# A fifth turn of the down-projection's second group as seven block products

## The chip, the core and the metric

The kernel runs on one core of one Trainium2 chip. The time is the device time of one execution in microseconds (us). The engines named below are TensorE (PE: matmuls; PEld: its weight loads), VectorE (DVE), ScalarE (ACT), GpSimd (POOL) and SyncE (SP, which issues most loads). Stores to DRAM are issued by SP and ACT and carried by 16 DMA engines.

## What is computed

The reference is two residual blocks over 256 tokens of width 2048, in float32. The change touches only the very last product of the second block, the down-projection:

```python
h2 = rmsnorm_2(x, norm2_g[l])
u = causal_dwconv(jnp.einsum('bsd,df->bsf', h2, w_up[l]), conv_w[l], conv_b[l])
u_gate, u_val = u[..., :D_FF], u[..., D_FF:]
x = x + jnp.einsum('bsf,fd->bsd', jax.nn.silu(u_gate) * u_val, w_down[l])
```

Here `f = silu(u_gate) * u_val` is 256 x 5632, `w_down` is 5632 x 2048, and the result is added to `x` and stored.

## The kernel before

**Precision.** Every float32 operand is split into a high and a low part in the type that TensorE multiplies fast (fp32r). A product is three matmuls: high by high, high by low, low by high. ScalarE writes the high part of a piece of weights (`high_of_chunk`, `w_hi`, L1014), VectorE subtracts it from the piece to get the low part (`low_of_chunk`, `w_lo`, L1432).

**Items.** The weights come as pieces of 256 rows by 512 columns (512 KB), and the whole kernel is one list, `ITEMS`, each item with one split into `w_hi` and `w_lo`. These have four slots: item n is split when item n-4 has been multiplied (ACT waits for it). VectorE and ScalarE go through the same loop of steps; step n of a phase prepares item n+4 (`split`) and then does what else is to be done at that step. Below, the items of the phase `down` are counted from 0 (0 to 108 before the change).

**The down phase.** It has two groups of 1024 output columns (column blocks 0 and 1, then 2 and 3). The 5632 rows are 11 turns of 512 rows. A plain turn is 4 items, C0 to C3, of 12 matmuls each: 128 tokens by 128 rows by 512 columns, for 2 row tiles, 2 token tiles and 3 parts (`wide_chunk`, L653). A turn by products takes the 2 x 2 blocks of the piece (two token tiles, two halves of rows, two column blocks) by Winograd's scheme with 7 products instead of 8. Each product is an item of 6 matmuls (`wide_product`, L676 and L680); they are written P1 to P7 here. It needs:

- the four weight blocks in buffers of their own (`load_block` on SP), of which VectorE makes four differences (`block_sum`, L1437, 128x1024 each);
- sums of the turn's rows of `f`: VectorE adds high and low part (L1519), makes four sums (L1522 to L1525), ScalarE takes their high part two steps later (`sums_high`, L1074), VectorE their low part three steps later (`sums_low`, L1474). `SUMS_AT` has the step for each such turn, `SUM_TURNS` the turn, `down_wide` the place of the parts;
- P1, P5, P6 and P7 are summed over all turns of a group in four PSUM banks of their own (`XS`). After P6 of the group's last turn by products, ScalarE copies the sum of P1 (`first_product`, L1112) and VectorE adds all of them up and into `x` (`add_products`, L1670 to L1680: four steps with two instructions of 128x512 each, the first step being that of P6). The results of the other products and of the plain turns are in `GG`.

A turn by products is interleaved with a plain one, in the order `MIXED`:

```python
MIXED = (1, "C0", 5, 7, "C1", 6, 3, "C2", 4, 2, "C3")
```

`(8, 6)` in `WIDE_STEPS` is such a mixed stretch of 11 items and 90 matmuls: turn 8 plain, turn 6 by products. `(7, None)` is a plain turn. Before the change, the second group is items 53 to 108: (3, 0) 53 to 63, (7, None) 64 to 67, (4, 1) 68 to 78, (5, 2) 79 to 89, (8, 6) 90 to 100, turn 9 plain 101 to 104, turn 10 plain 105 to 108. The stretches of the profile that are shown below begin with items 68, 79, 90 and 101.

**The end.** When the last item that writes a column block is done, VectorE adds the block to `x` one item later (L2018), and ACT issues its store of 512 KB (L1415). For column block 2 that is after item 106. For column block 3 the last item does its first token tile first; VectorE adds it (L2030) and SP stores 256 KB (L535), then the second tile in two halves (L2034), stored with 128 KB each by ACT (L1417) and SP (L537).

**Places.** `f_hi` has 4 KB for each turn from y+0 on, `f_lo` from y+44 KB on; the sums of turn 6 lie where turn 3 was.

Of the kernel before, what the change touches and what calls it, by code (L numbers as in the profile page):

```python
# [58 lines left out]
for _name, _w in (("a_norm", KD), ("norm1", KD), ("norm2", KD), ("b_s", GROUPS),  # L59
# [29 lines left out]
    "out1": (((0, None), (1, None), (6, None), (2, 4), (3, 5), (7, None)),  # L89
             ((0, None), (1, None), (2, 4), (3, 5), (6, None), (7, None))),  # L90
    "down": (((3, None), (4, None), (8, None), (9, None), (5, 0), (6, 1), (7, 2), (10, None)),
             ((3, 0), (7, None), (4, 1), (5, 2), (8, 6), (9, None), (10, None))),
    "gm0": (((0, 3), (1, 2)),),
    "gm1": (((0, None), (1, 3), (2, None)),),
    "out2": (((0, None), (2, 1), (3, None)),) * 2,
}


SUM_TURNS = {"v": (3, 2), "out1": (4, 5), "down": (0, 1, 2, 6), "gm0": (3, 2), "out2": (1,)}


SUMS_AT = {"v": (4, 8), "out1": (1, 4), "down": (3, 6, 9, 64), "gm0": (-8, -5), "out2": (-7,)}

PLAIN = ("C0", "C1", "C2", "C3")
MIXED = (1, "C0", 5, 7, "C1", 6, 3, "C2", 4, 2, "C3")
# [57 lines left out]
def product_item(phase, g, turn, p):  # L163
    return ITEM_AT[Item(phase, g, p, turn, None, None)]
# [6 lines left out]
def last_by_products(phase, g):  # L171

    return [turn for name, group, turn in QUADS if (name, group) == (phase, g)][-1]
# [17 lines left out]
def sum_slot(phase, turn):  # L191

    return SUM_TURNS["gm0" if phase == "gm1" else phase].index(turn)


def sums_ahead(phase):

    return sum(len(turns) for name, turns in SUM_TURNS.items() if FIRST_ITEM[name] < FIRST_ITEM[phase])


def own_ahead(phase, g=0):

    return sum((FIRST_ITEM[name], group) < (FIRST_ITEM[phase], g) for name, group in GROUPS_BY_PRODUCTS)
# [59 lines left out]
def build(nc, x, x_tokens, stream, w_s, params, gain_rows, final_rows, gate_w, identity, consts, out):  # L263

    kib = 1024
# [23 lines left out]
    class Wide:  # L289
# [3 lines left out]
        def __init__(self, sb, name, blocks, hi, lo, rows, sums, u):  # L293
# [98 lines left out]


    down_wide = Wide(sb, "d", [("mix", 0), ("mix", 4 * kib), ("y", 88 * kib), ("y", 92 * kib)],
                     [("h", 0), ("h", 4 * kib), ("h", 8 * kib), ("y", 12 * kib)],
                     [("h", 12 * kib), ("h", 16 * kib), ("h", 20 * kib), ("y", 56 * kib)], ("h", 24 * kib), ("h", 28 * kib),
                     ("h", 24 * kib))
    out1_wide = Wide(sb, "o", [("mix", 0), ("mix", 4 * kib), ("x", 12 * kib), ("x", 4 * kib)],
                     [("h", 8 * kib), ("h", 12 * kib)], [("h", 24 * kib), ("h", 28 * kib)], ("h", 0), ("h", 16 * kib),
# [51 lines left out]
    sem = Sems()  # L451
# [20 lines left out]
    with block:  # L472
# [520 lines left out]
        def _(act):  # L993
# [75 lines left out]
            def sums_high(phase, n):  # L1069

                if n - 2 in SUMS_AT[phase]:
                    i = SUMS_AT[phase].index(n - 2)
                    act.wait_ge(sem["sums_ready"], sums_ahead(phase) + i + 1)
                    activation(wide[phase].sums_hi[i][:], wide[phase].sums[:], ACT.Copy).then_inc(sem["sums_hi_ready"], 1)  # L1074

            def first_product(phase, n):

                for name, g in GROUPS_BY_PRODUCTS:
                    if name != phase:
                        continue  # L1080
                    turn = last_by_products(phase, g)
                    if n == product_item(phase, g, turn, 6):
                        act.wait_ge(mm_done, product_item(phase, g, turn, 1) + 1)
                        if phase == "out1" and g == 0:

                            act.wait_ge(sem["v_lo_ready"], GROUPS)
                        elif phase == "out1":

                            act.wait_ge(sem["own_read"], own_ahead(phase, g))
                            act.wait_ge(sem["sq_ready"], 4)  # L1090
                        elif phase == "gm0":

                            act.wait_ge(sem["m_done"], M_HEADS)
                        elif phase == "gm1":

                            act.wait_ge(sem["merged_turned"], 2)
                        elif phase == "out2" and g == 0:

                            act.wait_ge(mm_done, FIRST_ITEM["out2"])
                        elif phase == "out2":  # L1100
                            act.wait_ge(sem["own_read"], own_ahead(phase, g))
                        elif phase == "v":

                            act.wait_ge(sem["x_sq_ready"], 2)
                            act.wait_ge(group_read[0], g)
                        elif g == 0:

                            act.wait_ge(sem["sums_lo_ready"], sums_ahead(phase) + 3)
                        else:
                            act.wait_ge(sem["own_read"], own_ahead(phase, g))  # L1110
                            act.wait_ge(sem["sums_lo_ready"], sums_ahead(phase) + 4)
                        activation(wide[phase].p1[:], XS[:, 0, :], ACT.Copy).then_inc(sem["p1_ready"], 1)  # L1112

            def v_taken(q):
# [23 lines left out]
            for n in range(items_of("v")):  # L1138
                for q in range(2):
                    if n == half_end("v", 0, q):  # L1140
                        v_taken(q)
                split("v", n)
                if n == 0:
                    in_high(3, 8, 12)
                if n == 1:
                    in_high(4, 12, 16)
                if n in (3, 6):
                    t = n // 6
                    act.dma_start(x_first[:, t, :], x_tokens[:, t, :]).then_inc(sem[f"x_first_in{t}"], 16)
                if n == 4:  # L1150
                    act.dma_start(ident[:], identity).then_inc(sem["ident_in"], 16)
                sums_high("v", n)
                if n in (11, 12):
                    t = n - 11
                    act.wait_ge(sem[f"x_first_in{t}"], 16)
                    activation(x_junk[:, t, :], x_first[:, t, :], ACT.Square,
                               accum_out=n_sum[:, t:t + 1]).then_inc(sem["x_sq_ready"], 1)
                if n == 12:
                    act.dma_start(ws_t[:], w_s).then_inc(sem["ws_in"], 16)
                first_product("v", n)  # L1160
                if n in gelu_at:
                    act.wait_ge(sem["scale_ready"], 1)
                    v_gelu(gelu_at[n])
                if n - 1 in gelu_at:
                    v_squares(gelu_at[n - 1])
# [44 lines left out]
            for n in range(items_of("out1")):  # L1210
                split("out1", n)
                if n == 0:
                    act.wait_ge(sem["v_lo_ready"], GROUPS)
                    act.dma_start(xt[:], x_tokens).then_inc(sem["x_again"], 16)
                    act.dma_start(final_row[:], final_rows).then_inc(sem["final_in"], 16)
                sums_high("out1", n)
                if n == 4:
                    y_high(GROUPS - 1)
                first_product("out1", FIRST_ITEM["out1"] + n)
                for q in range(2):  # L1220
                    at = n - out1_second - 1 - 3 * q
                    if at == 0:
                        act.wait_ge(sem["x_turned"], q + 1)
                        gained_high(norm_mid, q, TR)
                    if at in (1, 2):
                        squares(q, at - 1)
# [101 lines left out]
            for p in range(2):  # L1328
                gm, pa, pm = f"gm{p}", f"pa{p}", f"pm{p}"
                for n in range(items_of(gm)):  # L1330
                    split(gm, n)
                    if p and n == 1:
                        merged_high(1)
                    first_product(gm, FIRST_ITEM[gm] + n)
                for n in range(8):
                    split(pa, n)
                    if n in (1, 3):
                        h = n // 2
                        act.wait_ge(group_read[h], group_of(gm, h)[2])
                        by_token(gate_m[h], gate_m[h], ACT.Tanh, scale_half).then_inc(sem["gate_m_ready"], 1)  # L1340
                for n in range(8):
                    split(pm, n)
                    if n == 6:
                        merged_high(2 * p)
                    if p:
                        sums_high("out2", n - 8)
# [73 lines left out]
        def _(dve):  # L1420
# [51 lines left out]
            def low(to, of, hi, count, value, after):  # L1472
                dve.wait_ge(sem[count], value)
                return v.tensor_tensor(to, of, hi.bitcast(F32), ALU.subtract).then_inc(sem[after], 1)  # L1474
# [38 lines left out]
            def sums_of_rows(phase, n, a_hi, a_lo):  # L1513

                if n in SUMS_AT[phase]:
                    i = SUMS_AT[phase].index(n)
                    at_i = slice(4 * SUM_TURNS[phase][i], 4 * SUM_TURNS[phase][i] + 4)
                    rows, sums = wide[phase].rows, wide[phase].sums
# [8 lines left out]
            def sums_low(phase, n):  # L1527
                if n - 3 in SUMS_AT[phase]:
                    i = SUMS_AT[phase].index(n - 3)
                    low(wide[phase].sums_lo[i][:], wide[phase].sums[:], wide[phase].sums_hi[i][:], "sums_hi_ready",  # L1530
                        sums_ahead(phase) + i + 1, "sums_lo_ready")
# [600 lines left out]
```

## Time and profile before

| | us |
|---|---|
| median of 3 runs | 2097.87 |
| lowest and highest | 2097.71, 2098.06 |
| the profiled execution: its own time | 2097.71 |
| the profiled execution: span from first to last instruction | 2095.9 |
| TensorE busy, VectorE busy, ScalarE busy (of the span) | 2089.8, 1506.6, 1112.4 |

How to read it: the profile is of one execution. Matmuls are pipelined, so that their shown duration (0.39 us) is longer than the distance from one to the next; the rate is read from the distance of their starts. A row of the timeline has the start, the duration, the engine, the line of the kernel, the operation, output and inputs and their count; behind it in brackets stands how long the engine was idle before it and what ended that. Times are from the start of the span.

### The profile page before, as it was taken

The page shows a single profiled execution, that of the slowest core. Times are in us where ns is not written, and L with a number is a line of the kernel's source. Part 1 is how long each engine was busy: PE and PEld are TensorE (multiplying, and loading weights), DVE is VectorE, ACT ScalarE, POOL GpSimd, SP SyncE. Part 2 cuts the span into 40 slices and gives each one's busy share as a digit, 9 for nine tenths or more (in the row PEclk, how much of TensorE's full clock was granted, in tenths as well). Part 3 has the DMA queues.
Part 4 walks back from the last instruction along what each step waited for, and adds up shares of the span by engine and source line. Part 5 has one row for each costly group of instructions (what it writes and reads, how often), then busy time and mean ns, then how long its engine had stood idle before and what let it go on. Part 6 is the DMA issues. An engine that isn't in the chain of part 4 may idle for free.

```text
span 2095.9 us, 25218 instructions
## 1 busy us (share of the span) xinstructions
PE 2089.8 (100%) x10000; PEld 1750.1 (84%) x10000; DVE 1506.6 (72%) x1702; ACT 1112.4 (53%) x1314; POOL 17.5 (1%) x17
## 2 busy tenths in 40 slices
PE   9999999999999999999999999999999999999999
PEld 7888888888888887888888888888888888888887
DVE  7987656655787754665669678867777777779986
ACT  6765444444456544555455454555555555555553
POOL 0000000000000000100000000000000000000000
PEclk9999999999999999999999999999999999999999
DMA  8665555555764555544465656556556566556663
GB/s 337 210 200 175 198 187 187 194 187 189 272 214 157 194 194 171 177 155 153 150 210 181 221 169 208 167 185 192 187 185 195 183 192 190 181 181 232 224 203 133
DMA packets 111957, 404.40 MB, mean 193 GB/s; under 512 B 12512, under 2 KB 13280, under 8 KB 111328
## 3 DMA queue, kind: packets, MB, share of 16 engines
q1 hardware_dynamic: 109440, 394.66, 57.1%
q10 hardware_dynamic: 2400, 8.14, 1.0%
q8 instruction: 79, 1.29, 0.3%
q14 instruction: 38, 0.31, 0.0%
HBM read 400.65 MB, written 2.10 MB: 192 GB/s over the span
## 4 chain that ended last, share of the span: by engine, by line
PE 96%; DVE 3%; ACT 1%; DMA 0%; issue 0%; ACTq 0%; DVEq 0%
PE g L556 37%; PE g L653 23%; PE xs L581 8%; PE g L581 8%; PE xs L676 5%; PE xs L585 4%; PE g L585 4%; PE g L680 4%; DVE w_lo L1432 1%; PE xs L604 1%; PE xs L713 1%; ACT w_hi L1014 0%; PE xs L833 0%; DMA xf<-in_x 0%; PE xs L830 0%
## 5 line engine op out<-in xcount | busy, mean ns | idle before, releaser
L1432 DVE TENSOR_TENSOR w_lo<-raw,w_hi 128x1024 fp32r<-128x1024 f32 x659 | 803.4, 1223 | 492.6 <-ACT w_hi L1014 486.9
L1014 ACT ACTIVATE w_hi<-raw 128x1024 fp32r<-128x1024 f32 x659 | 697.4, 1059 | 756.6 <-PE g L556 411.7
L556 PE MATMUL g<-w_hi,mid_both 128*128 128x512 f32 x1024 | 326.7, 394 | 0.0
L556 PE MATMUL g<-w_hi,in_both 128*128 128x512 f32 x1024 | 318.8, 390 | 0.1
L556 PEld LDWEIGHTS g<-w_hi,in_both 128*128 128x128 f32 x1024 | 192.2, 188 | 40.3 <-DVE v_all L1564 0.5
L556 PEld LDWEIGHTS g<-w_hi,mid_both 128*128 128x128 f32 x1024 | 192.3, 188 | 39.6
L556 PE MATMUL g<-w_lo,mid_both 128*128 128x512 f32 x512 | 199.4, 389 | 0.0
L556 PE MATMUL g<-w_lo,in_both 128*128 128x512 f32 x512 | 199.2, 389 | 0.0
L581 PE MATMUL g<-mlp_both,w_hi 128*128 128x512 f32 x704 | 176.8, 393 | 0.0
L581 PE MATMUL xs<-mlp_both,w_hi 128*128 128x512 f32 x704 | 176.3, 392 | 0.0
L581 PEld LDWEIGHTS g<-mlp_both,w_hi 128*128 128x128 f32 x704 | 126.5, 189 | 22.8
L581 PEld LDWEIGHTS xs<-mlp_both,w_hi 128*128 128x128 f32 x704 | 126.6, 189 | 22.6
L653 PE MATMUL g<-w_hi,in_both 128*128 128x512 f32 x352 | 112.6, 390 | 1.3 <-DVE w_lo L1500 1.0
L556 PEld LDWEIGHTS g<-w_lo,in_both 128*128 128x128 f32 x512 | 96.1, 188 | 19.7
L556 PEld LDWEIGHTS g<-w_lo,mid_both 128*128 128x128 f32 x512 | 96.3, 188 | 19.1
L585 PEld LDWEIGHTS g<-mlp_both,w_lo 128*128 128x128 f32 x704 | 96.2, 190 | 7.0
L585 PEld LDWEIGHTS xs<-mlp_both,w_lo 128*128 128x128 f32 x704 | 96.0, 190 | 6.9
L585 PE MATMUL g<-mlp_both,w_lo 128*128 128x256 f32 x704 | 98.3, 282 | 0.0
L585 PE MATMUL xs<-mlp_both,w_lo 128*128 128x256 f32 x704 | 98.2, 282 | 0.0
L653 PE MATMUL g<-w_hi,f_hi 128*128 128x512 f32 x240 | 93.7, 390 | 0.2
L653 PE MATMUL g<-w_hi,f_lo 128*128 128x512 f32 x240 | 93.4, 389 | 0.0
L653 PE MATMUL g<-w_lo,f_hi 128*128 128x512 f32 x240 | 93.4, 389 | 0.0
(404 smaller groups left out, 3044.3 us busy)
## 6 DMA issues: line engine op xcount, KB each, us to landing
raw<-in_stream SPq DMA_DIRECT2D x659, 512.0 KB, 3.5
d_block<-in_stream SPq DMA_DIRECT2D x28, 512.0 KB, 4.6
o_block<-in_stream SPq DMA_DIRECT2D x24, 512.0 KB, 4.7
v_block<-in_stream SPq DMA_DIRECT2D x20, 512.0 KB, 4.4
gm_block<-in_stream SPq DMA_DIRECT2D x12, 512.0 KB, 5.1
x_first<-in_x_tokens ACTq DMA_DIRECT2D x2, 1024.0 KB, 6.8
gain_row<-in_gain_rows SPq DMA_DIRECT2D x8, 256.0 KB, 3.5
xt<-in_x_tokens ACTq DMA_DIRECT2D x1, 2048.0 KB, 8.0
```

The lines of the kernel that those rows point to most:

```text
L556: ins = mm(G[buf][:, t, :], a[:, kt, at_t], w[:, slot, j * COLS:(j + 1) * COLS], start=(kt == 0 and n == 0), stop=(last and j == ROWS_PER_ ...
L581: mm(UP[buf][:, b, :, :], w_hi[:, slot, j * COLS + b * P:j * COLS + (b + 1) * P], a_both[:, :, kt, :], start=(kt == 0), stop=False, skip_g ...
L585: ins = mm(UP[buf][:, b, 0, :], w_lo[:, slot, j * COLS + b * P:j * COLS + (b + 1) * P], a_both[:, 0, kt, :], start=False, stop=(last and j ...
L604: ins = turn(TR[:, b, t * P:(t + 1) * P], of[:, t, b * P:(b + 1) * P], ident[:])
L653: ins = mm(GG[:, bank, :], a[:, kt, t * P:(t + 1) * P], w[:, slot, half_chunk(j)], start=n == 0 and opens(item, bank), stop=ended and n == ...
L676: ins = mm(XS[:, own[p], :], a, w[:, slot, half_chunk(j)], start=first and opens_own(item), stop=last and j == 1 and n == 2, skip_group_ch ...
L680: ins = mm(GG[:, RESULT_OF[p], :], a, w[:, slot, half_chunk(j)], start=first and opens(item, RESULT_OF[p]), stop=False, skip_group_check=True)
L713: ins = mm(SV[:, t, :], w[:, t, :], a[:, t, :], start=(n == 0), stop=(n == 2))
L1014: activation(w_hi[:, n % RING, :], of[:], ACT.Copy).then_inc(hi_ready, 1)
L1432: v.tensor_tensor(w_lo[:, n % RING, :], of, w_hi[:, n % RING, :].bitcast(F32), ALU.subtract).then_inc(lo_ready, 1)
```

## The change

Turn 9 of the second group is computed as seven block products, interleaved with turn 10 in one mixed stretch of 11 items: items 101 to 111 are P1, C0, P5, P7, C1, P6, P3, C2, P4, P2, C3. The sums of turn 9's rows are made by VectorE at step 70, which is inside the mixed stretch (4, 1), and their parts go where turn 7's rows of `f` lie (y+28 KB and y+72 KB). Turn 9 becomes the last turn by products of the group, and so the own products are added up after its P6 (item 106) instead of after turn 6's (item 95). The last item that writes column block 2 is now item 110. ScalarE's copy of P1's sum waits for the fifth low part of sums, since it lies over the place where they are made.

```diff
@@ -89,17 +89,17 @@
     "down": (((3, None), (4, None), (8, None), (9, None), (5, 0), (6, 1), (7, 2), (10, None)),
-             ((3, 0), (7, None), (4, 1), (5, 2), (8, 6), (9, None), (10, None))),
+             ((3, 0), (7, None), (4, 1), (5, 2), (8, 6), (10, 9))),
...
-SUM_TURNS = {"v": (3, 2), "out1": (4, 5), "down": (0, 1, 2, 6), "gm0": (3, 2), "out2": (1,)}
-
-
-SUMS_AT = {"v": (4, 8), "out1": (1, 4), "down": (3, 6, 9, 64), "gm0": (-8, -5), "out2": (-7,)}
+SUM_TURNS = {"v": (3, 2), "out1": (4, 5), "down": (0, 1, 2, 6, 9), "gm0": (3, 2), "out2": (1,)}
+
+
+SUMS_AT = {"v": (4, 8), "out1": (1, 4), "down": (3, 6, 9, 64, 70), "gm0": (-8, -5), "out2": (-7,)}
...
@@ -392,8 +392,8 @@
     down_wide = Wide(sb, "d", [("mix", 0), ("mix", 4 * kib), ("y", 88 * kib), ("y", 92 * kib)],
-                     [("h", 0), ("h", 4 * kib), ("h", 8 * kib), ("y", 12 * kib)],
-                     [("h", 12 * kib), ("h", 16 * kib), ("h", 20 * kib), ("y", 56 * kib)], ("h", 24 * kib), ("h", 28 * kib),
+                     [("h", 0), ("h", 4 * kib), ("h", 8 * kib), ("y", 12 * kib), ("y", 28 * kib)],
+                     [("h", 12 * kib), ("h", 16 * kib), ("h", 20 * kib), ("y", 56 * kib), ("y", 72 * kib)], ("h", 24 * kib), ("h", 28 * kib),
                      ("h", 24 * kib))
...
@@ -1108,7 +1108,7 @@
                             act.wait_ge(sem["own_read"], own_ahead(phase, g))
-                            act.wait_ge(sem["sums_lo_ready"], sums_ahead(phase) + 4)
+                            act.wait_ge(sem["sums_lo_ready"], sums_ahead(phase) + 5)
                         activation(wide[phase].p1[:], XS[:, 0, :], ACT.Copy).then_inc(sem["p1_ready"], 1)
```

## Rows read from the trace of the kernel before

**Rows 1.** The page: granted clock in 40 slices, and the chain that ended last, by engine.

```profile
PEclk9999999999999999999999999999999999999999
...
PE 96%; DVE 3%; ACT 1%; DMA 0%; issue 0%; ACTq 0%; DVEq 0%
```

**Rows 2.** Busy time by stretch: length, then each engine's, clock, DMA share, GB/s.

```profile
2009.24:2030.09 20.85, 20.70 (x91) 16.81 (x90) 19.09 (x18) 11.65 (x12) 0.00 (x0) 1.00 0.57 202
2030.09:2050.49 20.40, 20.40 (x91) 16.89 (x90) 17.75 (x16) 11.57 (x11) 0.00 (x0) 1.00 0.62 206
2050.49:2070.89 20.40, 20.40 (x91) 16.89 (x90) 19.40 (x20) 11.94 (x12) 0.00 (x0) 1.00 0.35 117
2070.89:2092.66 21.77, 21.77 (x97) 17.83 (x95) 10.84 (x11) 5.30 (x5) 0.00 (x0) 1.00 0.33 108
```

**Rows 3.** VectorE in order of time, 2005 to 2027: start, duration, instruction.

```profile
2005.30 1.22 DVE L1519 TENSOR_TENSOR d_rows<-f_hi,f_lo 128x1024 f32<-128x1024 f32 x1
...
2008.15 1.22 DVE L1432 TENSOR_TENSOR w_lo<-raw,w_hi 128x1024 fp32r<-128x1024 f32 x1
...
2015.09 1.22 DVE L1432 TENSOR_TENSOR w_lo<-raw,w_hi 128x1024 fp32r<-128x1024 f32 x1
...
2018.69 1.22 DVE L1432 TENSOR_TENSOR w_lo<-d_block,w_hi 128x1024 fp32r<-128x1024 f32 x1
2019.82 1.22 DVE L1432 TENSOR_TENSOR w_lo<-raw,w_hi 128x1024 fp32r<-128x1024 f32 x1
2020.96 2.36 DVE L1432 TENSOR_TENSOR w_lo<-d_block,w_hi 128x1024 fp32r<-128x1024 f32 x2
...
2026.01 1.23 DVE L1432 TENSOR_TENSOR w_lo<-d_block,w_hi 128x1024 fp32r<-128x1024 f32 x1 [1.49 <-ACT w_hi L1014]
```

**Rows 4.** TensorE in order of time: items 71 to 72, 75 and 96.

```profile
2015.83 0.39 PE L676 MATMUL xs<-w_hi,d_sums_lo 128*128 128x512 f32 x1
2016.36 0.50 PE L653 MATMUL g<-w_hi,f_hi 128*128 128x512 f32 x1
...
2021.94 0.39 PE L653 MATMUL g<-w_hi,f_hi 128*128 128x512 f32 x1
...
2061.38 0.39 PE L680 MATMUL g<-w_hi,d_sums_hi 128*128 128x512 f32 x1
```

**Rows 5.** ScalarE in order of time: the high part of the sums.

```profile
2008.27 1.06 ACT L1074 ACTIVATE d_sums_hi<-d_sums 128x1024 fp32r<-128x1024 f32 x1 [0.41 <-DVE d_sums L1525]
```

**Rows 6.** VectorE in order of time: the additions, and the last results.

```profile
2063.88 0.68 DVE L1670 TENSOR_TENSOR d_u<-xs,d_u 128x512 f32<-128x512 f32 x1
...
2065.20 1.22 DVE L1432 TENSOR_TENSOR w_lo<-raw,w_hi 128x1024 fp32r<-128x1024 f32 x1
2066.34 0.68 DVE L1673 TENSOR_TENSOR d_u<-xs,d_u 128x512 f32<-128x512 f32 x1
...
2071.26 0.68 DVE L1679 TENSOR_TENSOR d_u<-xs,d_u 128x512 f32<-128x512 f32 x1
...
2072.82 3.50 DVE L1432 TENSOR_TENSOR w_lo<-raw,w_hi 128x1024 fp32r<-128x1024 f32 x3
...
2092.86 0.76 DVE L2034 TENSOR_TENSOR xw<-g,xw 128x256 f32<-128x256 f32 x2 [0.67 <-PE g L653]
```

**Rows 7.** The end: stores, last matmul, and stretches with DMA share and GB/s.

```profile
2088.68 0.54 ACTq L1415 DMA_DIRECT2D out<-xw  x1
...
2092.43 0.39 PE L653 MATMUL g<-w_hi,f_lo 128*128 128x512 f32 x1
...
2093.64 0.34 SPq L537 DMA_DIRECT2D out<-xw  x1
...
2089.50:2090.00 0.50, 0.50 (x4) 0.42 (x3) 0.00 (x0) 0.00 (x0) 0.00 (x0) 1.00 0.22 86
2090.00:2090.50 0.50, 0.50 (x4) 0.42 (x3) 0.00 (x0) 0.00 (x0) 0.00 (x0) 1.00 1.04 393
...
2095.00:2095.50 0.50, 0.00 (x0) 0.00 (x0) 0.00 (x0) 0.00 (x0) 0.00 (x0) 1.00 0.02 4
```

## The prediction

> **What bounds the kernel now.** I read the page first, for its clock line and its chain by engine [rows 1]: the clock stands at its top level throughout, and 96% of the chain that ended last is TensorE. Then the stretches of the down phase [rows 2], cut where its matmuls begin: a mixed stretch of 90 matmuls takes 20.40 us and the last 96 plain ones take 21.77 us, so a 512-column matmul costs 0.2267 us, one behind the other. Only the stretch from 2009.24, also 90 matmuls, takes 20.85 us. The timelines say why [rows 3, 4]: VectorE ran without a pause from the row sums at 2005.30 on, the low part of item 72 began at 2015.09, and its first matmul could start only at 2016.36, 0.53 us after the one before it. So TensorE sets the time, except where VectorE has more to do than TensorE's time over the same items: there VectorE's order decides. Therefore I went through VectorE's timeline at the three places where the change puts or moves its work, and then through the end [rows 5 to 7].
>
> **What the change does to each part.**
>
> *Matmuls.* Turn 9 of the second group had 4 items of 12 matmuls and gets 7 of 6: 6 fewer. 6 x 0.2267 = **-1.36 us** [rows 2]. That is the whole gain; the whole stretch of turns 9 and 10 goes from 96 matmuls to 90.
>
> *Splits and block differences.* 3 more items mean 3 more high parts on ScalarE (1.06 us) and 3 more low parts on VectorE (1.22 us); there are 4 block differences (1.22 us) besides. All are prepared during items 97 to 107. The same set was prepared for turn 6 out of the stretch before it, and the stretches from 2030.09 and 2050.49 both take 20.40 us [rows 2], with no time lost. VectorE is 17.75 us busy in the first of the two, which carries just this load. I cost them at nothing; the cover is TensorE's 20.40 us. Turn 6's stretch becomes lighter by the additions that leave it (eight instructions, [rows 6]) and heavier by turn 9's preparation. If VectorE's start-to-start time of 1.14 us did not hold there, 15 operations of 1.22 us would still be 18.3 us, below 20.40.
>
> *Loads.* Four 512 KB blocks come as blocks instead of as ring rows: same bytes. They are issued by SP behind items 93, 96, 98 and 99, as in the stretches before. Nothing else stands on SP's queue there but the remaining ring loads. I take zero for it.
>
> *The sums of rows at step 70.* This is the first time that they stand inside a mixed stretch. Step 70 prepares the low part of item 74, and the sums come before that of item 75. Before, these two stand at 2018.69 and 2019.82 [rows 3]. The sums and their four small operations take from 2005.30 to 2008.15, 2.85 us until the next low part [rows 3]. So item 75's low part starts at 2019.82 + 2.85 = 2022.67. From the start of a low part to the matmul that waits for it are 1.27 us (2015.09 to 2016.36), so item 75 starts at 2023.94. It started at 2021.94 [rows 4]: **2.00 us late**. Behind the shorter stall the matmuls also ran slow for a moment: the stretch lost 0.45 us [rows 2], of which the gap is 0.53 - 0.23 = 0.30; the remaining **0.14 us** I add again. No idle time of VectorE can take up any of it: it has none before this point, and its next is 1.49 us ahead of 2026.01, which is too late.
>
> The two waits that come with it: ScalarE's high part of the sums starts 2.97 us after the sums began (2008.27 against 2005.30, [rows 5]), so at 2022.79; queued behind it is item 77's high part, ready at about 2024.9, when VectorE arrives for item 77's low part (2022.67 + 2 x 1.14 = 2024.95). VectorE's low part of the sums (1.14 us) stands between items 77 and 78 and item 79's low part comes at about 2028.4 instead of 2026.01, 2.4 us later, while TensorE is 2.14 us later. That 0.25 us is covered by VectorE's lead in the next stretch, which lost nothing [rows 2]. The sums are ready 28 items before turn 9 needs them. The place y+28k is free: turn 7's rows were last read by item 67, which ended at 2009.24.
>
> *The additions of the own products.* The eight additions move from turn 6's items 95 to 98 to turn 9's items 106 to 109. Before, they lay under 12 following items; now only 5 items follow. With the end of P6 as the zero (2061.38 before, [rows 4]): the first addition starts at +2.50, its pair lasts 1.32, a low part 1.14 [rows 6]. Item 111's low part is the last, since no item follows it. So the third pair starts at +2.50 + 1.32 + 1.14 + 1.32 = +6.28, where two low parts no longer push it back, the fourth at +7.61, and from its start to the next operation are 1.56 (2071.26 to 2072.82): +9.17. Only then comes the addition of column block 2. That block is now finished by item 110, not two plain items before the end, so its addition too (1.22) is at the very end. Then block 3's first tile (+10.31, after the 1.14 of start-to-start) and its two halves from +10.9; they need 0.78 us until the last store is issued (2092.86 to 2093.64, [rows 6, 7]): +11.7. The last matmul starts at +1.36 + 2.72 + 1.36 + 1.36 + 2.49 = +9.29. Before, the last store was issued 1.21 us after the start of the last matmul (2092.43 to 2093.64); now it is 2.4 us: **1.20 us** more. Item 111's low part ends at about +5, its matmuls start at +6.80, so VectorE does not hold up TensorE here.
>
> *The stores.* Before, block 2's store (512 KB) was issued at 2088.68 and long done when the others began. Now it is issued at about +10.4, next to the 256 KB and two of 128 KB. A store runs at 393 GB/s with the DMA engines wholly busy [rows 7], so they do not overlap, they share. 1.05 MB take 2.71 us. The data of the 512 KB store began about 1.2 us after its issue (86 GB/s in the half microsecond to 2090.00 is its last 0.11 us); so from +11.6 to +14.3. Without the store of block 2 in the way the last data would end as before, some 1.4 us behind the last issue (all but nothing moves after 2095.00), at +13.1. **1.25 us** more; by the bound from below, if the order of the queues lets the short stores slip between, 0; by the one from above, all of 1.36 (the store's 512 KB). I take 1.25, because the end waits for all of them and the bytes have to pass.
>
> That the ACT and SP queues share is also what the Trainium skill says ("DMA: Bandwidth & Descriptors", Issuing engines are not separate DMA queues): they run on the same 16 engines. By its 436 GB/s (same page, Anatomy of one DMA) the 1.05 MB would take 2.4 us and the sum would be 0.3 us lower, an estimate; the trace's 393 decides.
>
> **Sum.** -1.36 + 2.00 + 0.14 + 1.20 + 1.25 = **+3.2 us** on the profiled execution (span 2095.9, its own time 2097.71): 2100.9. The median of the three runs is 0.16 above that execution: **2101.0 us**, 0.15% slower. The bound of what a measurement can tell here is 0.2%, 4.2 us: so no measurable change, on its slow side.
>
> **The rivals.**
>
> *The stores do not collide* (below 0.3 us). For it: the 512 KB store is issued some 1.3 us ahead of the last. Against it: DMA share at 1.0 and more during each store [rows 7]. Then +1.95: 2099.8. Chance 0.17.
>
> *VectorE hides the sums: the other side.* One mechanism, at item 75: if its low part were 2.85 us or more ahead of its matmuls, nothing would stall. It is 0.85 us ahead (low part from 2019.82, usable at 2021.09, matmuls at 2021.94). Even then only the 2.14 us go: +1.1 (2098.9) with the end as worked out, and -1.36 (2096.5) if the end is hidden as well. For it speaks only that VectorE is idle in the plain stretches; against it [rows 3]. Chance 0.05. Neither is faster by 4.2 us.
>
> *The clock falls behind the stall.* The 0.3 us gap left the clock at 1.00 in its stretch [rows 2], and no row shows a gap of 2 us. If TensorE fell from 2.4 to 1.2 GHz, a matmul would take 0.45 us, and each item of 12 done at that level costs 2.7 us more: one item gives 2103.7, over the bound. The Trainium skill ("TensorE: Matmul & The Clock Gate", HAM oscillation) says that a TensorE left waiting long enough is throttled; by its rule a gap as short as this, with full work around it, leaves the clock alone. Chance 0.04.
>
> *The backlog is carried on.* If VectorE's 1.14 us for the low part of the sums is not covered by what it gains on TensorE before item 83, there is a second stall of up to 1.1 us: 2102.1. Against it the 17.75 us busy of 20.40 in the next stretch. Chance 0.06.
>
> *The change does what it says and no more is lost than the gain* (an end that hides the additions, stall as worked out): +0.8, 2098.7. Against it [rows 6]: VectorE's additions cannot start before P6. Chance 0.04.
>
> **How the numbers follow.** The forecast itself has 0.64: the stall and the end are each read from an instance of the same operations, and their errors are some 0.3 us each, so its own range is 2100.3 to 2101.7. The range of 8 in 10 leaves out the hidden sums, the clock and half of the backlog's case: 2099.3 to 2102.1. More than 4.2 us slower is reached by the clock's case and by errors of 1 us upward, together 0.10. Faster by more than 4.2 us has no case, 0.01. The rest is 0.89.
>
> **What will show it.** In the stretch of turns (4, 1): 20.85 + 2.14, about 23.0 us, the wait of the matmuls of item 75 for the low part about 2 us, clock 1.00. The next two stretches 20.40 each. The last 90 matmuls 20.4 us without a gap. Between the start of the last matmul and the end of the span 5.9 us instead of 3.5; VectorE busy without a pause from P6 to the last store; the stores side by side. The prediction is wrong if the stall at item 75 is below 1.5 us, if another one follows, or if the start of the last matmul is less than 4.7 us ahead of the end of the span.

## The result and the profile after

The changed kernel took 2101.54 us in the median of 15 runs (2101.26 to 2103.24), the kernel before 2097.92 us (2097.71 to 2098.21, 15 runs). The ratio is 1.0021, with a 95% interval of 1.0014 to 1.0027: slower, by 0.14% to 0.27%. No run of the one kernel overlaps with one of the other. The median is 3.6 us above, and the forecast was 3.2. But the runs do not lie around their median. Sorted, in us:

```
2101.26 2101.33 2101.44 2101.49 2101.53 2101.54 2101.54 2101.54
2102.71 2102.93 2103.00 2103.09 2103.22 2103.24 2103.24
```

Eight runs have a mean of 2101.46, seven of 2103.06: two levels, 1.6 us apart. The ratio of the medians is 1.0017; the mean over all 15 is 2102.21, 0.20% above before, at the 0.2% that the prediction took as its bound. The profiled execution (its own time 2101.26, span 2099.2) is of the lower level, so it shows only the part that the sum describes.

The stretches of the changed kernel, cut at the first matmuls of items 68, 79, 90 and 101 and at the end of the last item (length, then the busy time of PE, PEld, DVE, ACT and POOL with their instructions, clock, DMA share, GB/s); they answer to [rows 2]:

```profile
2009.13:2032.11 22.98, 21.00 (x91) 16.73 (x90) 22.61 (x24) 12.47 (x13) 0.00 (x0) 1.00 0.55 183
2032.11:2052.51 20.40, 20.40 (x91) 16.89 (x90) 17.85 (x16) 11.58 (x11) 0.00 (x0) 1.00 0.64 206
2052.51:2072.91 20.40, 20.40 (x91) 16.89 (x90) 17.75 (x16) 11.56 (x11) 0.00 (x0) 1.00 0.64 206
2072.91:2093.31 20.40, 20.40 (x91) 16.70 (x89) 19.23 (x21) 8.75 (x9) 0.00 (x0) 1.00 0.00 1
```

Turns 9 and 10 take 20.40 us instead of 21.77: the gain is there, all of it. The next two stretches are full. The first, (4, 1), grew from 20.85 to 22.98 us, with VectorE busy 22.61 of them. VectorE's timeline there (low part of item 74, the sums, low part of item 75):

```profile
2018.56 1.22 DVE L1432 TENSOR_TENSOR w_lo<-d_block,w_hi 128x1024 fp32r<-128x1024 f32 x1
2019.69 1.22 DVE L1519 TENSOR_TENSOR d_rows<-f_hi,f_lo 128x1024 f32<-128x1024 f32 x1
...
2022.54 1.22 DVE L1432 TENSOR_TENSOR w_lo<-raw,w_hi 128x1024 fp32r<-128x1024 f32 x1
```

and TensorE's, the last matmul of item 74 and the first of item 75:

```profile
2021.59 0.39 PE L680 MATMUL g<-w_hi,d_sums_lo 128*128 128x512 f32 x1
2023.82 0.50 PE L653 MATMUL g<-w_hi,f_hi 128*128 128x512 f32 x1 [1.83 <-DVE w_lo L1432]
```

The sums push the low part back by 2.85 us, and the matmul starts 1.28 us after the low part's start. Between the two matmuls are 2.23 us where 0.23 would be: 2.00 us lost, a stall of the matmuls. The clock of this stretch is 1.00, but the 12 matmuls of item 75 take 2.85 us (2023.82 to 2026.67) instead of 2.72: the 0.13 us behind the stall.

The end, as a timeline of all engines but the weight loads:

```profile
2092.13 0.69 DVE L1680 TENSOR_TENSOR xw<-xw,d_u 128x512 f32<-128x512 f32 x1
...
2092.97 1.23 DVE L2018 TENSOR_TENSOR xw<-g,xw 128x1024 f32<-128x1024 f32 x1
2093.09 0.39 PE L653 MATMUL g<-w_hi,f_lo 128*128 128x512 f32 x1
2094.11 0.68 DVE L2030 TENSOR_TENSOR xw<-g,xw 128x512 f32<-128x512 f32 x1
2094.22 0.54 ACTq L1415 DMA_DIRECT2D out<-xw  x1
2094.71 0.75 DVE L2034 TENSOR_TENSOR xw<-g,xw 128x256 f32<-128x256 f32 x2
...
2095.48 0.34 SPq L537 DMA_DIRECT2D out<-xw  x1
```

The last matmul starts at 2093.09. VectorE is only then at the addition of column block 2, and the last store is issued 2.39 us later, against 1.21 before [rows 7]. From there to the end of the span it takes another 3.7 us, against 2.3. The stretches behind it show the four stores side by side (the last three columns: clock, DMA share, GB/s):

```profile
2095.25:2095.50 0.25, 0.00 (x0) 0.00 (x0) 0.20 (x1) 0.00 (x0) 0.00 (x0) 1.00 0.24 82
2095.50:2096.00 0.50, 0.00 (x0) 0.00 (x0) 0.00 (x0) 0.00 (x0) 0.00 (x0) 1.00 1.01 385
...
2097.50:2098.00 0.50, 0.00 (x0) 0.00 (x0) 0.00 (x0) 0.00 (x0) 0.00 (x0) 1.00 1.02 342
2098.00:2098.50 0.50, 0.00 (x0) 0.00 (x0) 0.00 (x0) 0.00 (x0) 0.00 (x0) 1.00 0.58 193
```

The DMA engines are full for 2.8 us without a break.

So the lower level was explained from the trace. Open were the upper level, and whether each part is what it seems. Three theories of the upper level: TensorE's clock falls behind the stall in some executions (the rival that the prediction gave 0.04); the four stores at the end cost more in some executions; something ahead of the down phase.

### The profile page after: what moved, and what is told of

Its sections match the earlier page's. It is cut to its first block, busy times and chain, and to the rows that moved or that the text cites. A ratio compares the mean times of both kernels' runs of the same rounds, so it can differ in the third digit from the quotient of the medians.

```text
span 2099.2 us, 25230 instructions
## 1 busy us (share of the span) xinstructions
PE 2089.6 (100%) x9994; PEld 1749.8 (83%) x9994; DVE 1518.2 (72%) x1715; ACT 1116.2 (53%) x1318; POOL 17.5 (1%) x17
## 4 chain that ended last, share of the span: by engine, by line
PE 95%; DVE 3%; ACT 1%; DMA 1%; issue 0%; DVEq 0%; ACTq 0%
PE g L556 37%; PE g L653 22%; PE xs L581 8%; PE g L581 8%; PE xs L676 5%; PE xs L585 4%; PE g L585 4%; PE g L680 4%; DVE w_lo L1432 1%; PE xs L604 1%; PE xs L713 1%; ACT w_hi L1014 1%; PE xs L833 0%; DMA raw<-in_stream 0%; DVE d_block L1437 0%
## 5 line engine op out<-in xcount | busy, mean ns | idle before, releaser
L1014 ACT ACTIVATE w_hi<-d_block 128x1024 fp32r<-128x1024 f32 x56 | 59.4, 1062 | 63.2 <-PE g L653 42.8
L653 PE MATMUL g<-w_hi,f_hi 128*128 128x512 f32 x224 | 87.6, 391 | 2.0 <-DVE w_lo L1432 1.8
L653 PE MATMUL g<-w_lo,f_hi 128*128 128x512 f32 x224 | 87.2, 389 | 0.0
```

Source lines behind the costliest of these rows:

```text
L653: ins = mm(GG[:, bank, :], a[:, kt, t * P:(t + 1) * P], w[:, slot, half_chunk(j)], start=n == 0 and opens(item, bank), stop=ended and n == ...
L1014: activation(w_hi[:, n % RING, :], of[:], ACT.Copy).then_inc(hi_ready, 1)
```

## The experiments

In the figures below "tail" is the time from the start of the last matmul to the end of the span, in the profiled execution: 3.50 us before, 6.15 us after. All ratios are against the kernel before on the same chip.

**e1: the changed kernel again.** No edit.

> The changed kernel once more, for its two levels: 8 of its 15 runs took 2101.3 to 2101.5 us, 7 took 2102.7 to 2103.2. Clock theory: TensorE's clock falls for a moment behind the 2 us stall at item 75 in some executions; both levels come again, 1.7 us apart, and a trace of the upper one shows a granted clock below 1.00 between items 75 and 85 and nowhere else before the last matmul. Store theory: the upper level comes from the four stores that share the DMA engines at the end; a trace of the upper one shows its 1.7 us behind the last matmul, and matmuls at 0.2267 us throughout.

Median 2101.84 (2101.46 to 2103.19, 11 runs), ratio 1.0019 (1.0010 to 1.0028). Eight runs from 2101.46 to 2102.09, three from 2102.91 to 2103.19. Two levels again, but the profiled execution was of the lower one, so the trace of an upper one was still missing.

**e2: turn 9's sums at step 60.** The sums of turn 0, at h+0 and h+12 KB, are read last by item 59; the place is free from then on.

```diff
-"down": (0, 1, 2, 6, 9)
+"down": (0, 1, 2, 9, 6)
-"down": (3, 6, 9, 64, 70)
+"down": (3, 6, 9, 60, 64)
-[("h", 0), ("h", 4 * kib), ("h", 8 * kib), ("y", 12 * kib), ("y", 28 * kib)],
-[("h", 12 * kib), ("h", 16 * kib), ("h", 20 * kib), ("y", 56 * kib), ("y", 72 * kib)]
+[("h", 0), ("h", 4 * kib), ("h", 8 * kib), ("h", 0), ("y", 12 * kib)],
+[("h", 12 * kib), ("h", 16 * kib), ("h", 20 * kib), ("h", 12 * kib), ("y", 56 * kib)]
```

> The changed kernel with turn 9's sums of rows made at step 60 instead of step 70, in the place of turn 0's sums, which item 59 has read last. VectorE is idle three times for 1.5 us around the steps 59 to 62. Stall theory: the 2.0 us stall at item 75 and the 0.14 behind it go, up to 0.5 us may come back at items 64 to 72: 2099.2 to 2099.7. By the clock theory the upper level goes too, all runs agree within 0.4 us, and the median is 2 to 3 us under that of the changed kernel. By the store theory the lower level falls by 2.1 but the second level stays 1.7 us above it. Rival to the stall theory (the stall is only moved to another item): no change, 2101.3.

Median 2099.43 (2099.23 to 2100.18, 11 runs), ratio 1.0007 (0.9999 to 1.0016). The median is 2.4 us under e1's, the lowest run 2.2 under e1's lowest. No run is 1.6 above the lowest. All waits of TensorE for VectorE from 1990 us on, as the profile counts them, first in the changed kernel, then in e2 (us in total, times, longest; PEld are the weight loads ahead of the matmuls):

```profile
PEld g L653 <- DVE w_lo L1432: 2.8, 2, 2.3
PE g L653 <- DVE w_lo L1432: 1.8, 1, 1.8
```

```profile
PEld g L653 <- DVE w_lo L1432: 0.6, 1, 0.6
PE g L653 <- DVE w_lo L1432: 0.2, 1, 0.2
```

The stall of item 75 is gone and has not moved elsewhere; what stays is item 72's, which is as old as the kernel before. The tail is 6.15 us as in the changed kernel, so the four shared stores alone do not make the upper level.

**e3: the last mixed stretch in another order.** From the changed kernel:

```diff
+MIXED_LAST = (1, "C0", 5, 7, "C1", 6, 2, 4, 3, "C2", "C3")
...
-MIXED_LATE if _name in ("gm1", "out2") else MIXED
+MIXED_LAST if (_name, _by_products) == ("down", 9) else MIXED_LATE if _name in ("gm1", "out2") else MIXED
```

> The changed kernel with the last mixed stretch in the order P1, C0, P5, P7, C1, P6, P2, P4, P3, C2, C3: column block 2 is finished 1.36 + 5.44 us before the last matmul instead of 2.7. Its addition then stands before the last pair of additions, and its store of 512 KB is issued about 1.6 us earlier. End theory: VectorE's own 1.2 us at the end stays, the 1.25 us of the shared stores goes: lower level 2100.0 to 2100.3, the last data of the stores 1.4 us behind the last issue. If the stores had cost nothing: 2101.3. By the clock theory the second level stays 1.7 us above, by the store theory it goes.

Median 2101.27 (2100.11 to 2103.00, 11 runs), ratio 1.0016 (1.0007 to 1.0025). The lowest run is 1.35 us under e1's lowest. The end of its timeline (lines are two further down than in the other kernels):

```profile
2093.07 0.54 ACTq L1417 DMA_DIRECT2D out<-xw  x1
...
2095.89 0.34 SPq L539 DMA_DIRECT2D out<-xw  x1
```

The 512 KB store is issued 2.82 us before the last one instead of 1.26, and the tail is 5.0 us instead of 6.15: 1.15 us were the shared stores. The last store is still issued 2.4 us behind the start of the last matmul (2093.51): VectorE's lateness is untouched, as expected. The runs spread from 2100.11 to 2103.00 without a clean gap between them, so the upper level has stayed, with a shorter end. That speaks against the store theory, though no trace of such a run was taken.

**e4: the sums alone.** The kernel before, where turn 9 is plain, with the fifth set of sums made at step 70 as in the change and read by nobody. The output is unaffected.

```diff
-"down": (0, 1, 2, 6)
+"down": (0, 1, 2, 6, 9)
-"down": (3, 6, 9, 64)
+"down": (3, 6, 9, 64, 70)
```

(and the two places and the `+ 5` of the change)

> The kernel before, with turn 9 plain, and the fifth set of sums of rows made at step 70 all the same, into turn 7's place, and used by nobody. Nothing else of the change is in it. Stall theory: 2097.9 + 2.14 = 2100.0, all of it between items 74 and 76. Clock theory: some runs 1.7 us above that, at 2101.7. Store theory: one level only. If the sums fitted under TensorE: 2097.9.

Median 2101.68 (2100.17 to 2102.79, 11 runs), ratio 1.0016 (1.0007 to 1.0024). Four runs from 2100.17 to 2100.51, seven from 2101.48 to 2102.79. Its profiled execution took 2101.94, of the upper level. TensorE around item 75:

```profile
2024.24 0.50 PE L653 MATMUL g<-w_hi,f_hi 128*128 128x512 f32 x1 [1.81 <-DVE w_lo L1432]
2024.57 0.39 PE L653 MATMUL g<-w_lo,f_hi 128*128 128x512 f32 x1
...
2025.28 0.63 PE L653 MATMUL g<-w_lo,f_hi 128*128 128x512 f32 x1
2025.70 0.63 PE L653 MATMUL g<-w_hi,f_lo 128*128 128x512 f32 x1
2026.13 0.63 PE L653 MATMUL g<-w_hi,f_hi 128*128 128x512 f32 x1
...
2028.27 0.57 PE L653 MATMUL g<-w_hi,f_lo 128*128 128x512 f32 x1
2028.68 0.40 PE L680 MATMUL g<-w_hi,f_hi 128*128 128x512 f32 x1
```

and the same kernel by stretch (the third column from the end is the granted clock):

```profile
2024.24:2025.28 1.04, 1.04 (x5) 0.85 (x5) 1.04 (x2) 1.04 (x2) 0.00 (x0) 0.98 0.31 35
2025.28:2028.26 2.98, 2.98 (x8) 2.34 (x7) 2.98 (x4) 0.75 (x1) 0.00 (x0) 0.50 0.77 245
2028.70:2032.00 3.30, 3.30 (x16) 2.69 (x15) 1.86 (x3) 2.12 (x2) 0.00 (x0) 1.00 0.93 361
```

One us after the matmuls resume, TensorE goes on at 1.2 GHz (0.50) for 3.4 us (2025.28 to 2028.68): the matmuls start every 0.43 us instead of 0.23, and then the clock is back. Eight matmuls at 0.2 us more each are the 1.6 us between the levels. The clock theory is shown: with turn 9 plain and the stores of the kernel before, the sums alone make both the stall and the upper level. It is not something ahead of the down phase either: up to 2024.24 the clock is 1.00, and the low part of item 74 starts only 0.42 us later than in the trace of the changed kernel (2018.98 against 2018.56).

The single runs say the same. The mean clock of each is known to three decimals; 3.4 us at half the clock are 0.0008 of this span. The four lower runs of e4 have 1.000, the seven upper ones 0.999. In the changed kernel all seven upper runs have 0.999, but so have three of the eight lower ones: with the longer end the clock can also fall behind the last matmul, inside the span, where it costs nothing (0.51 from 2098.50 us on in the changed kernel's own trace). No trace shows the changed kernel itself on the upper level.

**e5: both edits together** (e2 and e3).

> The changed kernel with both edits: turn 9's sums at step 60 in turn 0's place, and the last mixed stretch in the order P1, C0, P5, P7, C1, P6, P2, P4, P3, C2, C3. If the stall (with the clock behind it) and the end are separate terms, both gains add: 6 fewer matmuls (-1.36) against VectorE's own lateness at the end (+1.2): 0 to 0.3 us under or over the kernel before, and one level only. If the two hide each other (a later start of the end takes up the stall), the gain is less than 3.4 us from the changed kernel's lower level.

Median 2098.65 (2098.27 to 2099.06, 11 runs; before 2097.97), ratio 1.0003 (0.9994 to 1.0011), no change that can be told from noise. One level. The gains add to within 0.4: 2101.46 - 2098.27 = 3.2 us between the lowest runs of e1 and e5 (on different chips), where the two alone gave 2.2 and 1.35. It is 0.7 us above before, where 0.3 was the most expected. The tail is 5.0, 1.5 us more than before; VectorE's lateness is 1.2 of them (last store issued 2.40 behind the last matmul's start, 2091.33 to 2093.73). The other 0.3 I put down to the three small stores, which used to be issued 1.4 us apart (2092.22 to 2093.64) and now within 0.67 (2093.06 to 2093.73), so that they too share.

**e6: P6 sooner.** As e5, with P6 ahead of C1:

```diff
-MIXED_LAST = (1, "C0", 5, 7, "C1", 6, 2, 4, 3, "C2", "C3")
+MIXED_LAST = (1, "C0", 5, 7, 6, "C1", 2, 4, 3, "C2", "C3")
```

> As e5, but with P6 moved ahead of C1 in the last mixed stretch: P1, C0, P5, P7, P6, C1, P2, P4, P3, C2, C3. The additions may then start 2.7 us earlier against the last matmul. End theory: VectorE is done with them 1.2 us or more sooner, at most 0.4 us of its lateness stays, and the kernel is 0.9 to 1.3 us faster than before (ratio 0.9995). Rival: VectorE has not split P6 by then, TensorE waits for it within the stretch, and what is won at the end is lost there: no better than e5.

Median 2098.45 (2098.28 to 2098.78, 11 runs), ratio 1.0002 (0.9993 to 1.0011): no better than e5, so the 0.9 to 1.3 us expected did not come. The rival did not hold either: there is no new wait of TensorE. VectorE was nearly on time (last store issued 1.42 us behind the last matmul's start), but its addition of block 2 now stood behind all four pairs, where in e5 it came ahead of the last one (it starts at 2090.44, in e5 at 2089.66), and the 512 KB store was again only 1.25 us ahead of the last store. The tail was 5.2 us.

**e7 and e8: the length of the stall.** e4 with less and with more of VectorE's work at step 70; the sums are read by nobody.

```diff
 # e7: two of the four small sums left out at step 70
+if (phase, n) != ("down", 70):
     link(v.tensor_tensor(sums[:, 0], a21, a22, ALU.add))
     link(v.tensor_tensor(sums[:, 1], sums[:, 0], a11, ALU.subtract))
 # e8: high and low part added a second time at step 70
+if (phase, n) == ("down", 70):
+    link(v.tensor_tensor(rows[:], a_hi[:, at_i, :].bitcast(F32), a_lo[:, at_i, :].bitcast(F32), ALU.add))
```

> As e4 (the kernel before, and sums at step 70 that nobody uses), but two of the four small sums are left out at step 70, about 0.9 us of VectorE. The stall at item 75 should be about 1.1 us instead of 2.0, lower level 2099.3 to 2099.5. Clock theory: the clock falls the more rarely the shorter the stall is; at 1.1 us no upper level or one in fewer than 3 of 11 runs. Rival: the clock falls whenever there is a stall: half of the runs 1.6 us higher, as in e4.

> As e4, with the addition of high and low part made twice at step 70, 1.25 us more of VectorE. The stall at item 75 should be about 3.3 us: lower level 2101.3 to 2101.5 us. Clock theory: the clock falls in nearly every execution, 1.6 us more: 2102.9 to 2103.2, and one level again. Rival (half of the runs whatever the length): two levels, 2101.4 and 2103.0.

e7: median 2099.34 (2099.17 to 2100.76, 11 runs), ratio 1.0007 (0.9998 to 1.0015). e8: median 2102.82 (2101.34 to 2104.39, 11 runs), ratio 1.0021 (1.0012 to 1.0030). The matmul behind the stall, first in e7, then in e8:

```profile
2023.07 0.50 PE L653 MATMUL g<-w_hi,f_hi 128*128 128x512 f32 x1 [0.92 <-DVE w_lo L1432]
```

```profile
2025.39 0.50 PE L653 MATMUL g<-w_hi,f_hi 128*128 128x512 f32 x1 [3.10 <-DVE w_lo L1432]
```

With the matmul before it at 2021.77 and 2021.90, the stalls are 1.07 and 3.26 us. In e7 ten of 11 runs are within 0.8 us of the lowest and one is 1.6 above it. All 11 have a mean clock of 1.000, the high one too, so none of them had such a fall, and what made that one run long is not known. In e8 four are from 2101.34 to 2101.63, with a mean clock of 1.000, and six from 2102.65 to 2103.06, with 0.999. One is at 2104.39 with 0.998: by the clock and by the time, 3.05 us above the lowest, as much as two falls. The expectation of e7 held. That of e8 did not: the clock fell in 7 of 11, not in nearly all, and the two levels stand where its rival had them, 2101.4 and 2103.0. Its profiled execution is of the upper level, and shows the fall again:

```profile
2026.00:2027.00 1.00, 1.00 (x5) 0.85 (x4) 1.00 (x2) 1.00 (x2) 0.00 (x0) 0.82 0.61 205
2027.00:2028.00 1.00, 1.00 (x4) 0.74 (x3) 1.00 (x2) 0.18 (x1) 0.00 (x0) 0.50 0.91 332
```

**e9: block 2 ahead of the last pair.** As e6, with VectorE's addition of column block 2 one step earlier:

```diff
-if at_item == half_end("down", q // 2, q % 2) + 1:
-    dve.wait_ge(mm_done, at_item)
+if at_item == half_end("down", q // 2, q % 2) + (q < 2):
+    dve.wait_ge(mm_done, at_item + (q == 2))
```

> As e6, but the addition of column block 2 stands one step earlier, ahead of the last pair of additions. In e6 the span ended 5.18 us behind the start of the last matmul: VectorE was only 0.2 us late there, but the 512 KB store was issued at 2091.70, 1.25 us ahead of the last one. Store theory of the end: issued 1.6 us sooner it is out of the way, the end falls to about 3.8 us, and the kernel is 0.8 to 1.0 us faster than before, 2097.0 to 2097.3. If the end of e6 came from something else than the shared stores: 2098.4 as in e6.

Median 2097.49 (2097.15 to 2097.66, 11 runs; before 2097.96), ratio 0.9997 (0.9988 to 1.0006). The tail is 4.06 us. Where e6's came from is settled: the addition and the 512 KB store of block 2 moved, VectorE's lateness stayed (1.43), and 1.1 us came back. It is 0.5 us under before, less than the 0.8 expected, by the 0.3 of the small stores again. These are issued at 2092.16, 2092.50 and 2092.83, when the 512 KB are all but through; their own 512 KB then fill the DMA engines from 2093.0 to 2094.5:

```profile
2092.50:2093.00 0.50, 0.00 (x0) 0.00 (x0) 0.30 (x1) 0.00 (x0) 0.00 (x0) 1.00 0.16 57
2093.00:2093.50 0.50, 0.00 (x0) 0.00 (x0) 0.00 (x0) 0.00 (x0) 0.00 (x0) 1.00 0.99 365
2093.50:2094.00 0.50, 0.00 (x0) 0.00 (x0) 0.00 (x0) 0.00 (x0) 0.00 (x0) 1.00 1.01 350
2094.00:2094.50 0.50, 0.00 (x0) 0.00 (x0) 0.00 (x0) 0.00 (x0) 0.00 (x0) 1.00 0.99 324
```

In the kernel before, the 256 KB were through before the first 128 KB began.

**e10: the sums one step earlier.** As e9, with `SUMS_AT` at 59 and 63 instead of 60 and 64.

> As e9, with both sets of sums one step earlier, at 59 and 63. The 0.45 us that the stretch from item 68 loses in every kernel so far comes from the sums of turn 6 at step 64, which stand behind a block difference that VectorE waited 0.49 us for. Stall theory: one step earlier they use that idle time, and 0.4 to 0.5 us come back: 2096.6 to 2096.9. Rival: the loss only moves to another item, same time as e9.

Median 2097.09 (2096.69 to 2097.71, 11 runs), ratio 0.9996 (0.9987 to 1.0004). The stretch of items 68 to 78, which took 20.85 us before:

```profile
2009.06:2029.46 20.40, 20.40 (x92) 16.90 (x91) 17.75 (x16) 11.52 (x11) 0.00 (x0) 1.00 0.62 206
```

The old stall of item 72 is gone too, and from 1990 us on TensorE waits for VectorE nowhere. The median is 0.87 us under that of the kernel before, but the interval holds 1: a version better than the changed one by 4.4 us (medians, on two chips), while these runs do not show that it is better than the one before.

## Why the prediction was right in its sum and wrong in its verdict

- **The matmuls, -1.36:** as forecast, from 21.77 to 20.40 us.
- **Splits, block differences, loads at nothing:** right. The stretches around them take 20.40 us as before, though VectorE is 17.75 to 19.23 us busy in them.
- **The stall at item 75, 2.00 + 0.14:** right in both parts; the stretch lost 2.13 us more than before (22.98 against 20.85). e2 takes it away, e4 makes it by itself.
- **VectorE's lateness at the end, 1.20:** the last store is issued 2.39 us behind the last matmul's start instead of 1.21. e6 and e9, with P6 sooner, take away 1.0 of it (1.42 and 1.43).
- **The stores, 1.25:** the rest of the tail measured 1.47 us (6.15 - 3.50 - 1.18). 1.15 are the 512 KB store (e3), 0.3 the small ones among themselves, which the sum had left out. That term was 0.2 too small. Its own figures give 1.2 rather than 1.25 (data until +14.3 against +13.1), and the 393 GB/s that it took throughout was not held: 371 to 389 while the large store ran, 342 at the end.
- **Sum:** +3.2 forecast; the span grew from 2095.9 to 2099.2, 3.3 us. The median of the runs, 2101.54, lies in the range and 0.5 from the forecast.
- **The verdict:** "no measurable change" was wrong. The step that failed is the rival *The clock falls behind the stall*: its chance of 0.04, its price, and so its place outside the sum. The prediction argued that the 0.3 us gap left the clock alone and that no row shows a gap of 2 us, and took that for safety, where it only meant that nothing was known. By the times of the runs the clock fell in 7 of the 15 executions. Its price was set at 2.7 us for each item done at 1.2 GHz; it was 1.6 us in all, since only eight matmuls were. So a rival did not replace the forecast but came on top of it in half of the runs, and lifted their mean from 3.5 to 4.3 us above before, to the 0.2% itself. The Trainium skill ("TensorE: Matmul & The Clock Gate", HAM oscillation) would let a gap of this length pass; the trace of e4 shows that it does not always, and the measurement decides.
- **The bound of 0.2%:** a second weak step, worked out from no row. The sum said +3.2 us, and the prediction called that unmeasurable. Here the interval reaches about 1.4 us to either side, and the lowest run after is 3.05 us above the highest before. So even the lower level by itself, 3.5 us, was a slowdown that the runs can tell.

The median inside the range owes something to luck: with one more execution on the upper level it would have been 2102.7 or so, outside 2102.1.

What stays open: why the clock falls in one execution and not in the next of the same kernel. Counted by time and mean clock, it fell in 22 of 48 executions with the 2.0 us stall (7 of 15 and 3 of 11 of the changed kernel, 5 of 11 in e3, 7 of 11 in e4), in none of 11 at 1.07 us, and in 7 of 11 at 3.26. So a longer stall than 2.0 us did not make it clearly more frequent, and what decides it no run here shows. In e1 to e4 the runs also spread within a level, by about 1 us, which makes single counts of e3 unsure. Part of that comes from far ahead: e2's profiled execution, the longest of its runs, is already 0.84 us behind the kernel before at the same low part near 1992 us, with the clock at 1.00.

## What to carry to other kernels

Where one engine is full, new work on a helper engine is priced by its lead at that place, not by its busy share: 2.85 us of sums cost 2.0 us of matmuls at step 70 and nothing measurable at step 59, where VectorE had been idle for 1.5 us between two splits. A cut at the end of a program is paid back if it moves additions and stores behind the last matmul, so count what is issued after the last item's start, in bytes too. A stall of the matmul engine by 2 us can cost more than 2 us: look at the single runs, their times and their mean clock to the third decimal, for a second level before trusting the median or the one profiled execution.

## What the runs showed of the hardware that I had not expected

- After a stall of 2.0 us, inside otherwise unbroken work, TensorE's granted clock fell to 0.50 (1.2 GHz) for 3.4 us in 22 of 48 executions; after 0.3 and 1.07 us no run shows it. The fall came not in the gap but 1.0 us (e4) and 1.3 us (e8) after the matmuls had resumed. The matmuls then started every 0.43 us instead of 0.23; cost 1.6 us.
- The profiled execution can be of either level, and its mean clock tells only in the third decimal: 0.999 on the upper level, 1.000 on the lower one in e4 and e8. In the changed kernel three runs of the lower level have 0.999 too, so there only the time of the run tells.
- Three stores of 256, 128 and 128 KB took about 0.3 us more when issued within 0.67 us than within 1.4 us (e5 and e9 against the kernel before).
